# Moving three projection tiles out of an attention stage and into the projection before it

## The reference, cut to what matters

```python
h = rms_norm(x, norm_mix_pre)
# columns of h @ w_in, in this order:
#   c_q (384), c_kv (128), k_rope (32), gqa q (512), gqa k (128), gqa v (128), three gates (1024 each)
...
def mla_attention(c_q, c_kv, k_rope, positions, q_norm, w_uq, kv_norm, w_ukv):
    q = (rms_norm(c_q, q_norm) @ w_uq)      # 8 heads, 64 + 32 (rotated)
    kv = (rms_norm(c_kv, kv_norm) @ w_ukv)  # 8 heads, keys 64 and values 64
    ...                                     # full softmax attention over all 512 keys

def windowed_gqa(q, k, v, positions, sink):
    ...                                     # 8 query heads, 2 key/value heads, a band of 128 to each side
```

## Time and profile before

| | |
|---|---|
| median of 3 runs | 3058.34 us |
| the profiled execution: its own time | 3059.8 us |
| its span (first to last instruction) | 3058.0 us |
| mean granted TensorE clock | 0.972 of full |
| busy: TensorE (matmul) / VectorE / ScalarE / GpSimd | 2881.0 / 1513.2 / 1072.5 / 449.9 us |
| DMA | 245.80 MB, 80 GB/s mean |

### The profile page before, as it was taken

One profiled execution on the slowest core, in us unless ns is written; L12 is line 12 of the kernel. 1 busy time (PEld: TensorE's weight loads), 2 busy tenths in 40 slices (PEclk: granted clock), 3 DMA queues, 4 the chain that ended last, 5 costly groups with the idle time before them and its releaser, 6 DMA issues. The chain is left out here.

```text
span 3058.0 us, 34797 instructions
## 1 busy us (share of the span) xinstructions
PE 2881.0 (94%) x12356; PEld 2224.1 (73%) x12356; DVE 1513.2 (49%) x2229; ACT 1072.5 (35%) x1631; POOL 449.9 (15%) x283
## 2 busy tenths in 40 slices
PE   6998999899999899899999999989999998899998
PEld 4885567688887688546777888767677677578886
DVE  4356684433324534758444333354668735553333
ACT  4234433332223433443333222342443333432221
POOL 1010011311112301001121111230011113121101
PEclk9999999999999899999999999999999899999999
DMA  3221012222222222101222223222232122122232
GB/s 122 98 87 56 14 43 82 83 96 97 96 99 95 77 86 94 56 14 56 69 83 86 97 98 104 97 69 97 69 109 85 42 69 83 42 83 96 96 104 89
DMA packets 37047, 245.80 MB, mean 80 GB/s; under 512 B 4144, under 2 KB 5168, under 8 KB 7984
## 3 DMA queue, kind: packets, MB, share of 16 engines
q1 hardware_dynamic: 33600, 239.09, 22.9%
q10 hardware_dynamic: 3312, 4.93, 0.5%
HBM read 241.91 MB, written 2.10 MB: 80 GB/s over the span
## 5 line engine op out<-in xcount | busy, mean ns | idle before, releaser
L505 PE MATMUL bank<-h_hi,w_hi 128*128 128x512 f32 x2152 | 863.6, 401 | 39.3 <-DVE h_lo L1403 28.3
L507 PE MATMUL bank<-h_hi,w_lo 128*128 128x512 f32 x2152 | 844.7, 393 | 0.0
L506 PE MATMUL bank<-h_lo,w_hi 128*128 128x512 f32 x2152 | 844.7, 393 | 0.0
L1320 DVE TENSOR_TENSOR w_lo<-raw,w_hi 128x2048 fp32r<-128x2048 f32 x225 | 520.1, 2312 | 559.9 <-ACT w_hi L924 384.6
L505 PEld LDWEIGHTS bank<-h_hi,w_hi 128*128 128x128 f32 x2152 | 407.9, 190 | 149.0 <-issue 33.6
L507 PEld LDWEIGHTS bank<-h_hi,w_lo 128*128 128x128 f32 x2152 | 408.0, 190 | 86.4
L506 PEld LDWEIGHTS bank<-h_lo,w_hi 128*128 128x128 f32 x2152 | 408.3, 190 | 86.0 <-issue 4.6
L924 ACT ACTIVATE w_hi<-raw 128x2048 fp32r<-128x2048 f32 x137 | 261.8, 1911 | 313.5 <-PE bank L507 303.6
L505 PE MATMUL bank<-a_hi,w_hi 128*128 128x512 f32 x528 | 205.4, 389 | 0.0
L506 PE MATMUL bank<-a_lo,w_hi 128*128 128x512 f32 x528 | 205.4, 389 | 0.0
L507 PE MATMUL bank<-a_hi,w_lo 128*128 128x512 f32 x528 | 205.4, 389 | 0.0
(11 more groups left out here) (352 smaller groups left out, 3998.6 us busy)
## 6 DMA issues: line engine op xcount, KB each, us to landing
raw<-in_stream SPq DMA_DIRECT2D x226, 1024.0 KB, 4.9
x<-in_xT SPq DMA_DIRECT2D x2, 1024.0 KB, 11.8
out_T<-x ACTq DMA_DIRECT2D x8, 256.0 KB, 2.1
p_f<-in_pT ACTq DMA_DIRECT2D x2, 512.0 KB, 3.7
memf<-in_memT ACTq DMA_DIRECT2D x1, 1024.0 KB, 5.5
cst_sb<-in_cst ACTq DMA_DIRECT2D x1, 411.5 KB, 6.1
pos_i<-in_pos ACTq DMA_DIRECT2D x1, 258.0 KB, 8.7
vec<-in_vec ACTq DMA_DIRECT2D x2, 26.0 KB, 1.8
```

The source lines that it names most:

```text
L505: nc.tensor.matmul(ps, wh, xh, start=start, stop=False)
L506: nc.tensor.matmul(ps, wh, xl, start=False, stop=False)
L507: return nc.tensor.matmul(ps, wl, xh, start=False, stop=stop)
L1320: nc.vector.tensor_tensor(w_lo[s][:, :], raw[s][:, :], w_hi[s][:, :].bitcast(F32), ALU.subtract).then_inc(lo_ready, 1)
```

## The change

The stage `z1b` is gone. Its three tiles are tiles 8 to 10 of `z1`, which has now eleven; in the order of the tiles the value tile comes first of the banded ones (tile 6), then the four query tiles (7 to 10). Behind tile 10, and before `uq`, TensorE turns the value tile (tile count 11). ScalarE takes `vcT` out of tile 6; VectorE copies the four query tiles and then `vc`. `mla` has nothing between its items. The units per layer stay the same in number; the two that `z1b` had are now units 4 and 5 of `z1`, and their successors are split by ScalarE and VectorE, where GpSimd split two high parts during `mla`.

```diff
 TILES = {
-    "z1": plain_tiles(8, 8),
-    "z1b": plain_tiles(8, 3),
+    "z1": plain_tiles(8, 11),
...
-    stage("z1", A=5, SS=4), stage("qn", N=2, R=4), stage("uq", A=16),
-    stage("z1b", A=1, HP=1), stage("mla", I=32, H=8, O=4), stage("gqa", I=32, H=8, O=4),
+    stage("z1", A=6, SS=4), stage("qn", N=2, R=4), stage("uq", A=16),
+    stage("mla", I=32, H=8, O=4), stage("gqa", I=32, H=8, O=4),
...
                 run(c, "z1", normed, after=after_z1)
+                pe.wait_ge(act_took, c.at("A", "z1", 6))
+                ps = free_bank(c, "z1", 11)
+                for t in range(ST):
+                    mm = nc.tensor.transpose(ps[:, t * P:(t + 1) * P], vcT[:, t * P:(t + 1) * P], ident)
+                mm.then_inc(tile_done, 1)
...
-                attention(c, "mla", [(tile_free, c.at("T", "uq", 16)), (kr_copied, c.layer + 1)],
-                          lambda t: run_blocks(c, "z1b", normed, beside("z1b", t, 2)))
-                pe.wait_ge(act_took, c.at("A", "z1b", 1))
-                ps = free_bank(c, "z1b", 3)
-                for t in range(ST):
-                    mm = nc.tensor.transpose(ps[:, t * P:(t + 1) * P], vcT[:, t * P:(t + 1) * P], ident)
-                mm.then_inc(tile_done, 1)
+                attention(c, "mla", [(tile_free, c.at("T", "uq", 16)), (kr_copied, c.layer + 1)])
...
-                attention(c, "gqa", [(tile_free, c.at("T", "z1b", 4))], lambda t: run_blocks(c, "am", am, beside("am", t, 3)))
+                attention(c, "gqa", [(tile_free, c.at("T", "uq", 16))], lambda t: run_blocks(c, "am", am, beside("am", t, 3)))
...
+                        act.wait_ge(kr_copied, c.layer + 1)
+                        take_hi(c, "z1", 6, 5, vcT[:, :])
...
-                attention(c, "mla", also=lambda t: after_blocks(c, "z1b", beside("z1b", t, 2), evac_z1b))
+                attention(c, "mla")
...
+                    elif n == 6:
+                        dve.wait_ge(act_took, c.at("A", "z1", 6))
+                        pass_on(c, "z1", 6)
                     else:
-                        copy_out(c, "z1", n, n, qc[:, n - 6, :], lambda ps: ps[:, :], wait_act=False)
+                        copy_out(c, "z1", n, n, qc[:, n - 7, :], lambda ps: ps[:, :], wait_act=False)
                 stage_loop(c, "z1", evac_z1)
+                copy_out(c, "z1", 11, 0, vc[:, :, :], lambda ps: ps[:, :].rearrange("p (t d) -> p t d", t=ST), wait_act=False)
...
-                attention(c, "mla", also=lambda t: after_blocks(c, "z1b", t, 2, evac_z1b))
-                copy_out(c, "z1b", 3, 0, vc[:, :, :], lambda ps: ps[:, :].rearrange("p (t d) -> p t d", t=ST), wait_act=False)
+                attention(c, "mla")
...
-                split_units(c, "z1b")
                 split_units(c, "am")
...
-        blocks += column(rope, 0) + column(w_in, at_kc)
-        for m in range(2):
+        blocks += column(rope, 0) + column(w_in, at_kc) + column(w_in, at_vc)
+        for m in range(4):
             blocks += column(w_in, at_qc + m * P)
```

More of the change, by code:

```diff
@@ L139, in stage @@
         c["PU"] = sum(kind == "PU" for kind, _ in rel)
-        c["T"] = {"four1": 16, "four2": 5, "z1b": 4, "ple": KD + NO_TILES}.get(name) or len(TILES[name])
+        c["T"] = {"four1": 16, "four2": 5, "z1": 12, "ple": KD + NO_TILES}.get(name) or len(TILES[name])
         c["HP"] = c.get("HP", 0) * c["U"]
@@ L1147, in first_block @@
                                    bias=posf[:, S + b:S + b + 1]).then_inc(dist_ready, 1)
-                def evac_z1b(n):
-                    if n == 2:
-                        take_hi(c, "z1b", 2, 0, vcT[:, :])
-                attention(c, "mla", also=lambda t: after_blocks(c, "z1b", beside("z1b", t, 2), evac_z1b))
+                attention(c, "mla")
                 def gate_am(n):
@@ L2045, in lay_out @@
         put(blocks + wide(k_cols, range(1)) + wide(v_cols, range(1)))
-        put(column(w_in, at_qc + 2 * P) + column(w_in, at_qc + 3 * P) + column(w_in, at_vc))
         put(merge(w_in, at_gate, inputs["w_branch_a"][i], 4))
```

## The result

The changed kernel takes 3064.66 us (median of 20 runs, 3061.92 to 3067.50) against 3060.64 us for the kernel before, run beside it (20 runs, 3057.84 to 3062.31). The ratio is 1.0014, 95% interval 1.0008 to 1.0021: slower by some 4 us. That is clear of no change, though the ratio lies inside the 0.2% that the forecast called no change. I had forecast 3060.7 us, in a range from 3054.5 to 3068, and +2.4 us over the kernel before. The forecast started from 3058.34 us, the median of three runs; the twenty runs put the kernel before 2.3 us higher. So of the 4.0 us between forecast and measurement 2.3 are the base and 1.6 the cost of the change.

A forecast was written before the change was run, and what follows sets the result against it. TensorE, busy 94% of the span, was taken to bound the kernel. Per layer 16.3 + 0.7 - 11.6 (layer 2: 12.6) - 2.1 - 1.6 gave +1.7 and +0.7 us, together +2.4 on 3058.34: 3060.7 us, range 3054.5 to 3068.

The forecast's parts named there:

- The base: Starting time of the forecast sum: 3058.34 us, the median of the runs, 1.5 us below the profiled execution.
- z1 grows by 16.3 us: In z1, per layer: the 72 moved matmuls at 0.227 us each add 16.3 us, all on the path, without stall.
- rival D: In z1: a weight unit comes late, about 1 us a layer, 3063 us; the forecast with D has 0.53.
- Turning and copying v ahead of uq, +0.7: Ahead of uq: VectorE's copy of vc shifts its rotation chain by 0.7 us a layer, bounds 0.4 and 1.1.
- Items 0 and 1, hidden: Start of mla: the four blocks there were truly hidden, so taking them away gives nothing; logits 2 stay 7.4 us after logits 0.
- Items 2 to 14, -11.6 and -12.6: In mla, logits 2 to 15: without blocks 28.7 and 29.3 us, so -11.6 us in layer 1, -12.6 in layer 2.
- The end of mla, -2.07: Between mla and gqa, per layer: the transposes and the wait for the copy of vc go, -2.07 us.
- The clock at the start of gqa, -1.6 a layer: gqa's items 0 and 1: without the 1.42 us idle the clock does not fall, 7.58 us become 6.0, -1.6 a layer.
- B: In mla: all 72 matmuls had cost nothing there, so the change adds 30 us, 3088 us; chance 0.03.
- A: Start of mla: without blocks the clock rises late and first heads run at half rate, +12 us in all, 3070 us; chance 0.12.
- C: Start of mla, uq and gqa: mla runs without the low clock and uq has less of it, faster, 3051 us; chance 0.08.
- E: Start of gqa: the clock falls as before, so 1.6 us a layer are not won, 3063.9 us; chance 0.24.

The follow-up runs named there:

- the last version: Changed kernel with two query tiles taken out of z1, one behind mla's items 0 and 1, one in uq behind tile 8: 3038.52 us, ratio 0.9931 to the kernel before.
- few blocks: Kernel before with only 6 of the 24 z1b blocks per layer kept, the first and last of each tile: 3044.91 us, ratio 0.9958.
- v early: Kernel before with the value tile first in z1b and v turned behind item 14 of mla: 3057.83 us, ratio 0.9994.
- one tile: Changed kernel with the last query tile kept in mla, all behind items 0 and 1: 3052.91 us, ratio 0.9976 to the kernel before.

## Why the prediction was right, and where not

- *The base.* 3058.34 us, the median of three runs, was 2.3 us below the median of twenty. That the forecast was 4.0 us low is mostly this.
- *z1 grows by 16.3 us.* Right. From the start of the touched stretch to uq's first matmul it is 158.70 us before and 175.36 after, +16.67 with the transposes in all six layers, 0.35 of it the transposes (175.02 without them, in the version with v turned behind mla). No weight unit came late; rival D is out.
- *Turning and copying v ahead of uq, +0.7.* Nearly right. VectorE's first rotation stands 4.56 us after uq's first matmul in the first trace of the kernel before (213.67 in the earlier trace rows) and 4.81 us in that of the changed one (233.23), and the transposes had moved that matmul by 0.35 us: the chain shifted by 0.60 us. How much of it reaches uq's end is not shown: uq's mean grew by 0.20 us, while the clock spreads it by 1.4 us in both kernels. The rotation before and after:

```profile
218.23 0.69 DVE L1522 TENSOR_TENSOR rope_t<-bank,cs 32x512 f32<-32x512 f32 x1
```

```profile
238.04 0.69 DVE L1519 TENSOR_TENSOR rope_t<-bank,cs 32x512 f32<-32x512 f32 x1
```

- *Items 0 and 1, hidden.* Right: 7.39 us in every layer of every trace but the last version's.
- *Items 2 to 14, -11.6 and -12.6.* Measured -12.16 in the mean. The after side was forecast at 28.7 and 29.3 us and came at 27.7 to 28.8. In layer 1 that is two small errors against each other, which is luck: I gave this stretch 3.3 us of half clock and it had 6.8, so items 2 to 4 took 6.9 us, not 6.2; the ten items behind them with their values took 21.9 us, not 22.5. On the side of before, layer 2's 41.88 us was a single case; the other five layers have 40.3.
- *The end of mla, -2.07.* Measured 13.14 to 11.06, -2.08.
- *The clock at the start of gqa, -1.6 a layer.* This is the term that was mis-sized. That the clock would not fall without the idle time was right, in all six layers. But I took the first trace's two falls for what the kernel before always does. In its three traces it does so in three of six layers, which makes the gain 0.8 us a layer and the sum 2.4 + 1.6 = 4.0 us. The medians differ by 4.0 us and the touched stretches by 3.5. That the first fits so well is partly luck, since the share of one half rests on six layers. What decides in a layer whether the clock falls stays open.
- *Rivals.* B (the blocks were hidden) is out by the run that leaves most of them out. A (the first heads crawl) did not happen: the half clock ended within some 7 us of logits 2, and the first values come 15.7 us after them. C (mla without the low clock) did not happen either. E's 3063.9 us is the nearest to the measured time, but only because the base was low: against the kernel run beside it, +4.0 us lies midway between the forecast's +2.4 and E's +5.6. And E's mechanism is wrong: the clock does not fall in the changed kernel; it falls less often in the kernel before. The Trainium skill's rule there (TensorE: Matmul & The Clock Gate, "HAM oscillation — how this bites in real kernels"), that long idle gaps bring half rate, agrees with the traces: the changed kernel ran at half clock for 4.4 to 6.8 us after the 5.41 us gap ahead of logits 2, and blocks in the gap removed that (28.43 to 26.67 us). What I read into it, that a shorter gap is not the cause, is not borne out. With the 1.42 us gap the clock fell in four of twelve layers and without it in none of twelve; such a split would come by chance about once in twenty, so this is well supported and not proven. And in all six layers of the kernel before, half clock for 3.3 us or more followed a gap of 2.64 to 2.66 us ahead of logits 2.

What the forecast passed over is where the moved work could have gone. It named items 0 and 1 and uq's 3.72 us as idle, and one query tile in each of these two places gave a version some 26 us faster than the changed kernel.

## What to carry to other kernels

Work placed beside an attention is only free where the engine that does it waits. Compare an item with and without the filler before moving it either way: here 20 of 24 blocks cost nine tenths as much in mla as in a projection, while the 48 matmuls of two query tiles, put into two real gaps, cost nothing that the stages around them show, and gave back half clock besides. When a term of a sum rests on the clock at one place, take it from several executions; each layer of a trace is one sample, and two layers that agree are not yet a rule. Take the base of the sum from many runs too. A value that the next stage waits for at its door (here the turned v, 2.08 us) is cheaper ahead of a stage that does not wait for it (0.60 us ahead of uq).

## What the runs showed of the hardware beyond what I had expected

With the same instructions and the same 1.42 us of idle time ahead of gqa, the granted clock fell to 0.50 behind it in some layers and not in others: three of six in the kernel before, one of four with v turned late, none of two with few blocks. Without that idle time it fell in none of twelve (six of the changed kernel, two each with v early, with one tile and with two). When it fell, items 0 and 1 took 7.54 to 7.58 us, otherwise 6.01 to 6.03. A stage that no edit touched and in which TensorE stays busy repeats within 0.1 us from trace to trace and chip to chip (layer 1's feed-forward takes 298.56 to 298.61 us in all twelve). Stages in which it idles do not: the start 54.76 to 58.38 us, dsa 115.76 to 122.16 us. Two traces of kernels that differ by 4 us can thus differ by 7 for reasons that neither owns.
